# Two projections of a hybrid attention trunk: first tile and weights loaded by the phase before, waits on last stores moved, the opening's load order changed

## What is computed

```python
mod = silu(c) @ ada_w[layer] + ada_b[layer]              # six vectors of 1024, for latent and context tokens
h = rmsnorm(x, norm1_g) * (1 + scale) + shift             # the modulated input
# layer 0 (even): one input matrix, 2304 columns
qa, ka, va, qb, kb, vb = split(h @ ev_w_in)               # A: differential attention, B: windowed attention
# layer 1 (odd): one input matrix, 2336 columns
q_a, kv_a, k_r, nq, nk, nv = split(h @ od_w_in)           # C: low rank (512 + 256 + 32), D: neighbourhood
q = rmsnorm(q_a) @ wq_up ; kv = rmsnorm(kv_a) @ wkv_up    # 768 and 1024 columns
# heads are rms-normed (and turned by the rope tables), attended, projected, and followed by an MLP
```

## Time and profile before

| what | value |
|---|---|
| median of 3 runs | 3759.4 us (3757.71 to 3764.4) |
| the profiled execution, own time | 3761.42 us |
| its span in the trace | 3759.6 us |
| granted TensorE clock, mean | 0.961 |
| busy: PE, DVE, ACT, POOL | 93%, 58%, 36%, 5% |
| moved by DMA | 366.45 MB, mean 97 GB/s |

### The profile page before, as it was taken

One profiled execution on the slowest core, in us unless ns is written; L12 is line 12 of the kernel. 1 busy time (PEld: TensorE's weight loads), 2 busy tenths in 40 slices (PEclk: granted clock), 3 DMA queues, 4 the chain that ended last, 5 costly groups with the idle time before them and its releaser, 6 DMA issues. The chain is left out here.

```text
span 3759.6 us, 47907 instructions
## 1 busy us (share of the span) xinstructions
PE 3489.7 (93%) x17598; PEld 2847.5 (76%) x17598; DVE 2175.2 (58%) x3197; ACT 1339.8 (36%) x2435; POOL 185.1 (5%) x188
## 2 busy tenths in 40 slices
PE   6989898998999999999979799799899899999998
PEld 3867666886888888888858587577687678888887
DVE  5869665885755444554464355688787453333333
ACT  4533344664511111111145455566466331111111
POOL 1110300000300000000001000000000010000000
PEclk8999898998999999999989899899899999999999
DMA  6657465224322212222233444433363311111112
GB/s 222 203 201 240 120 133 135 57 75 124 90 79 58 63 57 71 69 68 58 68 101 135 167 131 123 98 73 86 65 127 76 113 51 48 47 50 50 51 50 68
DMA packets 433093, 366.45 MB, mean 97 GB/s; under 512 B 104469, under 2 KB 375077, under 8 KB 427813
## 3 DMA queue, kind: packets, MB, share of 16 engines
q1 hardware_dynamic: 432933, 364.36, 34.4%
HBM read 276.60 MB, written 87.69 MB: 97 GB/s over the span
## 5 line engine op out<-in xcount | busy, mean ns | idle before, releaser
L2470 DVE SCALAR_TENSOR_TENSOR xT<-ps,mods,xT 128x1024 f32<-128x1024 f32 x192 | 189.4, 1014 | 357.0 <-PE ps L2712 357.0
L3050 DVE TENSOR_TENSOR e_plain<-e_plain 128x1280 f32<-128x1280 f32 (+1 forms) x64 | 87.0, 1359 | 482.1 <-ACT e_plain L2899 482.1
L2712 PE MATMUL ps<-e_gh,e_w2h 128*128 128x512 f32 x1280 | 352.0, 372 | 5.9 <-DVE e_w2l L2988 3.6
L2712 PE MATMUL ps<-e_gl,e_w2h 128*128 128x512 f32 x1280 | 349.1, 370 | 0.0
L2712 PE MATMUL ps<-e_gh,e_w2l 128*128 128x512 f32 x1280 | 349.0, 370 | 0.0
L2899 ACT ACTIVATE e_plain<-ps 128x1280 f32<-128x1280 f32 (+1 forms) x64 | 72.7, 1135 | 722.9 <-PE ps L2712 718.8
L2712 PE MATMUL ps<-e_hl,e_w1h 128*128 128x512 f32 (+1 forms) x1200 | 327.2, 370 | 0.0
L2712 PE MATMUL ps<-e_hh,e_w1l 128*128 128x512 f32 (+1 forms) x1200 | 327.2, 370 | 0.0
L2712 PE MATMUL ps<-e_hh,e_w1h 128*128 128x512 f32 (+1 forms) x1200 | 327.2, 370 | 0.0
L2712 PEld LDWEIGHTS ps<-e_gh,e_w2h 128*128 128x128 f32 x1280 | 222.3, 188 | 55.2 <-DVE e_gl L3054 8.0
L2847 ACT CAST e_w2h<-e_raw 128x512 fp32r<-128x512 f32 x128 | 79.4, 620 | 495.5 <-PE ps L2712 495.5
(11 more groups left out here) (418 smaller groups left out, 7580.8 us busy)
## 6 DMA issues: line engine op xcount, KB each, us to landing
e_raw<-in_mlp_w SPq DMA_DIRECT2D x64, 512.0 KB, 4.2
e_raw<-in_mlp_w SPq DMA_DIRECT2D x128, 256.0 KB, 2.9
rstd<-in_ada_w SPq DMA_DIRECT2D x64, 384.0 KB, 3.4
e_raw<-in_w_out SPq DMA_DIRECT2D x40, 512.0 KB, 4.0
qkC<-pc_stage SPq DMA_DIRECT2D x72, 192.0 KB, 2.7
hT<-pb_hb SPq DMA_DIRECT2D x10, 1024.0 KB, 5.7
pa_hb<-hT SPq DMA_DIRECT2D x10, 1024.0 KB, 7.1
qkA<-pa_stage SPq DMA_DIRECT2D x20, 512.0 KB, 3.7
```

Of the source, the lines that this page charges most:

```text
L2470: ins = k.nc.vector.scalar_tensor_tensor(out=x, in0=ps, scalar=k.mods[:, layer, gate, bass.ds(n, 1), w], in1=x, op0=ALU.mult, op1=ALU.add)
L2712: mm = pe.matmul(k.ps[:, SB * (e % 2) + b, 0:n], w[:, e % 2, f], m[:, f, c0:c0 + n], start=(f == 0 and x == 0), stop=(f == nf - 1 and x == 2))
L3050: nc.vector.tensor_tensor(g, g, g, ALU.mult).then_inc(s.sqg, 1)
```

## The change

1. `ProjectionStart` and `LowRankStart` are new objects that hold fixed SBUF places and two semaphores (weights, tile). "pb" loads the first h tile and the first six slices of "pa"; "pd" loads the first h tile and all 16 slices of "pc"'s input matrix (3.3 MB) over the columns of its own unit 0, which its last two tiles don't use, and over its raw buffers.
2. `project` no longer waits for its stores at its end. It returns a function that does, and SP of the following block calls it just before `clear_before` ("pb" to "pa", "pa" to "ab", "pd" to "pc").
3. "pc" no longer has three raw buffers: the up matrices have places of their own. It cuts three kv slices before its first `low_rank`, and PE does `products(1)` right behind `products(0)`.
4. The opening has eight places for the eight groups of `ada_w`, so that no group waits; groups and x tiles alternate, all weight slices come behind them, and the orders of PE, ACT and DVE are written anew to follow. POOL makes the rope tables first, then the base of h tile 0, and takes half of its modulation.

```diff
+class LowRankStart:
+    def load_weights(self, sp):
+        for r in range(2):
+            for f in range(KT):
+                sp.dma_start(self.raw[r][f], self.w[r][f]).then_inc(self.weights, 16)
+    def load_tile(self, sp):
+        sp.dma_start(f32(self.hb[:, 0].rearrange("p a f q -> p (a f q)")), self.h).then_inc(self.tile, 16)
@@ opening @@
-        loads = [(0, 0, 0, None), (0, 1, 1, None), (1, 0, 2, None), (1, 1, 3, None), (2, 0, 0, 0), (2, 1, 1, 1), (3, 0, 2, "dve"), (3, 1, 0, 2)]
+        steps = [("ada", (0, 0)), ("x", 1), ("ada", (0, 1)), ("x", 2), ("x", 3), ("tables", 0), ("ada", (1, 0)), ("ada", (2, 0)), ("x", 4),
+                 ("ada", (2, 1)), ("x", 5), ("ada", (1, 1)), ("x", 6), ("ada", (3, 0)), ("x", 7), ("ada", (3, 1)), ("x", 8), ("x", 9)]
@@ opening, sync @@
-                for x in range(KT, len(slices)):
+                for x in range(len(slices)):
                     fetch_w(x)
@@ opening, tensor @@
+                ada(0, 0)
+                turn_x(1)
+                ada(0, 1)
+                turn_x(2)
+                turn_x(3)
+                ada(1, 0)
+                turn_rows(0)
+                turn_x(4)
+                ada(1, 1)
+                spread(0)
+                turn_x(5)
+                turn_x(6)
+                ada(2, 0)
+                turn_rows(1)
+                turn_x(7)
+                ada(2, 1)
+                vector_sums()
+                turn_rows(2)
+                turn_x(8)
+                turn_x(9)
+                spread(1)
                 spread(2)
@@ opening, scalar @@
+                    if x == 0:
+                        act.wait_ge(s.ada, 2)
...
-                    for f in range(KT):
+                    for f in range(KT // 2):
                         a = nc.scalar.activation(made.h[:, f], made.h[:, f], ACT.Identity, ...)
                     a.then_inc(s.fmod, 1)
                     act.wait_ge(s.fmod, 1)
+                    act.wait_ge(s.fmodp, 1)
                     nc.scalar.copy(made.hb[:, 0, 0], made.h[:]).then_inc(s.ht, 1)
...
+                for t in (5, 6, 7):
+                    take_x(t)
+                    square(t)
+                root(1)
+                square(8)
+                cut(0)
                 rows_out(2)
-                for x in range(4, RAW):
+                for x in (1, 2, 3):
                     cut(x)
                 modulate()
+                for t in (8, 9):
+                    take_x(t)
+                square(9)
+                root(2)
+                for x in (4, 5, 6, 7):
+                    cut(x)
                 take_rstd(1)
@@ opening, gpsimd @@
+                pool.wait_ge(s.base, 1)
+                pool.wait_ge(s.modd, 4)
+                pool.wait_ge(s.m0, 2)
+                for f in range(KT // 2, KT):
+                    a = nc.gpsimd.tensor_scalar(made.h[:, f], made.h[:, f], k.mods[:, 0, 1, f, 0:1], k.mods[:, 0, 0, f, 0:1], ALU.mult, ALU.add)
+                a.then_inc(s.fmodp, 1)
@@ project, sync @@
+                    if begun is None or x >= RAW:
+                        sp.dma_start(raw[:, x % RAW, 0:u.width], w_dram[...]).then_inc(wr[x % RAW], 16)
                     if x == RAW - 1:
+                        if stores_before is not None:
+                            stores_before(sp)
                         k.phases.clear_before(sp)
...
+                    if begins is not None and n == first_of[NT - 2] and not NG:
+                        sp.wait_ge(s.mm, first_of[NT - 2])
+                        sp.wait_ge(s.wlo, NW)
+                        begins.load_weights(sp)
+                    if begins is not None and n == first_of[NT - 1]:
+                        sp.wait_ge(s.mm, last_of[NT - 2] + 1)
+                        sp.wait_ge(hs[0], 16 * NT // 2)
+                        begins.load_tile(sp)
+                        if NG:
+                            sp.wait_ge(s.aacc, 2 * NG * KT)
+                            begins.load_weights(sp)
...
-                for p in range(2):
-                    sp.wait_ge(qd[p], 16 * ((len(head_jobs) + 1 - p) // 2))
-                    if value_jobs:
-                        sp.wait_ge(vd[p], 16 * ((len(value_jobs) + 1 - p) // 2))
-                    if keeps_h:
-                        sp.wait_ge(hs[p], 16 * NT // 2)
@@ project_low_rank, sync @@
-                fetch_h(0)
-                for x in range(len(slices)):
-                    fetch_w(x)
...
+                stores_before(sp)
+                for r in range(2):
+                    for f in range(RT[r]):
+                        sp.dma_start(up_raw[r][:, f], u_dram[r][f]).then_inc(wu[r], 16)
+                sp.dma_start(rope, k.ins["rope32"]).then_inc(s.ropec, 16)
+                fetch_h(1)
+                k.phases.clear_before(sp)
@@ project_low_rank, tensor @@
                 products(0)
+                products(1)
@@ project_low_rank, scalar and vector @@
-                for x in range(KT):
+                for x in range(KT + KV_EARLY):
                     cut(x)
                 low_rank(0)
```

More of the change, by code:

```diff
@@ L272, in __init__ @@
         self.rope = tile("rope", [P, 2, NT, HD])
-        last = units[-1]
-        assert prepared == len(units) - 1 and last.width == 512
-        self.spare = nc.alloc_sbuf_tensor_at(f"{name}_spare", [P, 2 * KT, n_cols], F32, offset=self.base)[:, :, last.c0:last.c0 + 512]
+        first, last = units[0], units[-1]
+        assert prepared == len(units) - 1 and first.width == last.width == 512
+        spare = nc.alloc_sbuf_tensor_at(f"{name}_spare", [P, 2 * KT, n_cols], F32, offset=self.base)
+        self.spare, self.spare_first = [spare[:, :, u.c0:u.c0 + 512] for u in (last, first)]
     def hold(self, nc, st, name):
@@ L369, in _ @@
                 sp.dma_start(brows[:], i["ada_b"].rearrange("l (k p) -> (l k) p", p=P)).then_inc(s.rows, 16)
-                for t in range(1, XB):
-                    fetch_x(t)
-                for y, (n, g, where, free) in enumerate(loads):
-                    if free == "dve":
-                        sp.wait_ge(s.aacc, 2 * GF)
-                    elif free is not None:
-                        sp.wait_ge(s.ada, free + 1)
-                    c = (n % 2) * HALF
-                    sp.dma_start(made.spare[:, GF * where:GF * where + GF], ada_w[n // 2, :, GF * g:GF * g + GF, c:c + HALF]).then_inc(aw_sem[where], 16)
-                    if y == 3:
+                for what, n in steps:
+                    if what == "x":
+                        fetch_x(n)
+                    elif what == "ada":
+                        n, g = n
+                        c = (n % 2) * HALF
+                        sp.dma_start(group(n, g), ada_w[n // 2, :, GF * g:GF * g + GF, c:c + HALF]).then_inc(aw_sem[2 * n + g], 16)
+                    else:
                         for j in hu:
@@ L523, in _ @@
                 square(0)
-                for t in range(1, XB):
+                take_x(1)
+                square(1)
+                rows_out(0)
+                for t in (2, 3):
                     take_x(t)
@@ L725, in turned_after, with landed @@
         return [n - LAG] if n - LAG in nth_head else []
+    def landed(x):
+        return wr[x % RAW], 16 * (x // RAW + (0 if begun is not None else 1))
     rest = [n for n in head_jobs if n + LAG >= N]
@@ L801, in fetch_vectors @@
                     sp.dma_start(raw[:, x % RAW], a_dram[a_group[a // KT], a % KT]).then_inc(wr[x % RAW], 16)
-                if not keeps_h:
+                if not keeps_h and begun is None:
                     fetch_h(0)
@@ L850, in products @@
                     if n == first_of[t]:
-                        if not keeps_h:
-                            pe.wait_ge(hl[t % 2], 16 * (t // 2 + 1))
+                        if begun is not None and t == 0:
+                            pe.wait_ge(begun.tile, 16)
+                        elif not keeps_h:
+                            pe.wait_ge(hl[t % 2], 16 * (t // 2 + (0 if begun is not None and t % 2 == 0 else 1)))
                         elif t >= tiles_ready:
@@ L921, in cut @@
                         x, u = nth_slice[j, f], units[j]
-                        act.wait_ge(wr[x % RAW], 16 * (x // RAW + 1))
+                        if begun is not None and x < RAW:
+                            act.wait_ge(begun.weights, 16 * RAW)
+                        else:
+                            act.wait_ge(*landed(x))
                         nc.scalar.copy(wh[:, f, u.c0:u.c0 + u.width], raw[:, x % RAW, 0:u.width]).then_inc(s.whi, 1)
@@ L1041, in vector_part @@
                     x, g, f = NW + a, a // KT, a % KT
[L1042 removed]
+                    dve.wait_ge(*landed(x))
                     if f:
@@ L1184, in project_low_rank @@
         gain = [k.rstd[:, 1152:1152 + D], sb("gain1", [P, D])[:]]
+        qh_at = next_free(nc)
+        qh = sb("qh", [P, 2, H, 2, D], F32R)
+        stage_at = next_free(nc)
+        stage = sb("stage", [D, 4, 4, P])
```

(5 more changed lines are left out.)

284 lines of the change are left out of this document (161 added, 123 removed).

## The result

The changed kernel takes 3729.7 us (median of 4 runs, 3724.2 to 3731.4) against 3759.9 for the kernel before: ratio 0.9916, 95% interval 0.9898 to 0.9933. That is faster by 30 us. It lies in the range of 3708 to 3731, but only 1.3 us under its end, and 11 of the 41 us that the terms promised are missing. The profiled execution took 3730.5 us, its span is 3728.7, so the two spans differ by 30.9. Further on one execution of one kernel, `edges_even`, is left out of its median: 3989.4 us at a mean clock of 0.825, where its others have 0.959 to 0.965.

A forecast was written before the change was run, and what follows sets the result against it. PE is busy 93% of the span, so time is won only where PE stands still or its clock is low. Terms -14 - 9 - 1 - 17 = -41 gave 3718 us, range 3708 to 3731.

The forecast's parts named there:

- The opening, -14: Opening: loads stream without group waits, so "pb" starts near 60 instead of 73.84 us, -14, bounds -9 to -17.
- PE has slack there of 2 to 3 us: Opening: PE's clock may be low after its wait for the third group, but PE has 2 to 3 us to spare.
- the start of the stream: Opening: loads run at 0.403 MB per us from near 3 us, the last x tile landing near 40.5.
- rival B: Opening: x tiles released late by waits on tile 4's transposes and squares; gain 7 instead of 14, 3725; chance 0.13.
- the case that the forecast had priced at some 2 us: Opening: POOL's four modulations could each stand behind a DVE cut, ending the opening some 2 us later.
- "pb" to "pa", -9: Edge "pb" to "pa": PE starts 7.8 us earlier, the last slice comes 8.8 earlier; -9, ends -7 and -10.
- "pa" to "ab", -1: Edge "pa" to "ab": the block starts 1.1 us earlier; -1, between 0 and -1.5.
- "pd" to "pc", -17: Edge "pd" to "pc": weights and tile loaded early, first up product 17.6 us earlier; taken as -17, bounds -12 to -20.
- Rival C: Start of "pc": its tile lands late, at 2133, so the gain is 11 instead of 17; 3724; chance 0.12.
- D: Slower: the queue serves mixed streams at about half of 403 GB/s, opening +9, in all about +5, 3764; chance 0.02.
- E: No effect: the shift is given back further on as DVE or a store paces "pa" and "pc"; 3759; chance 0.02.
- all else keeps its length: Phases behind the edges: a shift of the first tile should shift the rest, with later phases unchanged in length.

The follow-up runs named there:

- edges_even: Kernel before with only the edges "pb" to "pa" and "pa" to "ab" new, opening and edge to "pc" as before: -8.4 us by medians.
- opening_only: Kernel before with only the new opening and the moved "pb" weight issues, every edge as before: -7.0 us.
- half-width run: Changed kernel with PE's six conditioning half groups at 256 of their 512 columns: 3721.1 us (2 runs).
- late_clear: Changed kernel with the store wait and clears of "pa" moved on SP from behind its sixth weight slice to behind the twelfth: 3722.8 us.
- warm_pc: Changed kernel with POOL's wait for DVE's first low part, "pa"'s clears behind its twelfth slice, and 28 unread products at the start of "pc": 3724.8 us.
- warm_open: Changed kernel with unread products in the opening, 12 ahead of the fourth half group and 28 ahead of the second batch's spread: 3726.6 us.
- waits_moved: Changed kernel with both small edits: POOL's wait for DVE's first low part in "pb", and "pa"'s clears behind its twelfth slice: 3725.5 us.
- after_pool_waits: Changed kernel with POOL's product for tile 2 in "pb" waiting for DVE's first low part of tile 1: 3726.3 us.

## Why the prediction was right, and by how much each step was off

**The opening, -14: measured -7.0, in the profile -8.6.** ACT's queue from the row copy on was right: from `rows_out(2)` to the end of the last cut I had 16.6 us, measured 16.5 (47.92 to 64.41). The rate of a full stream was right too, 393 to 407 GB/s. The step that failed is "PE has slack there of 2 to 3 us". It had none. I had priced a half group at four records; there are eight, each 0.43 at full clock, 3.6 us. The row that showed it was in the trace of before (48 records for 24 products). PE ends its third pair at 47.9; I had ACT reach its row copy near 43.2 (41.4, a square, a cut), and the whole miss stands at that copy, 4.7 us.

Of the 4.7 us, 2.9 are the lower clock in one half group, as the run without that fall shows (44.99). The rest, 1.8 us, can't be given to the price alone: at the full clock weight slice 0 lands at 44.1, just ahead of ACT's `cut(0)`, so the transfers alone would hold the row copy until 44.7. I had x 9 land near 40.5 and slice 0 soon after, from a full rate since 3 us; with the slow windows ahead of 18 us x 9 lands at 43.4 and slice 0 at 44.1 even where nothing else is late (opening_only). So a second step was off, the start of the stream, by some 1.5 us, and it is hidden behind the first. The half-width run shows that PE was the path, and what comes next behind it.

Part of rival B came as well: in the changed kernel x 9 was released at 40.3 and landed at 44.9, because PE and so ACT's squares were late. But B had that as the cause, and here it is a consequence that held nothing: `cut(0)` started at 47.30 and did not wait for its slice. That the time is B's (3725) and not mine is no credit to either sum.

POOL's half cost 1.59 beyond ACT's, where I took 1. It is the case that the forecast had priced at some 2 us for all four modulations: the first of them stood 1.3 us behind DVE's cuts (1.76 against 0.45 us), the other three did not.

**"pb" to "pa", -9, and "pa" to "ab", -1: measured -8.0 and -1.3, together -8.4 by medians.** The part that I derived from PE's own start (-7.8) is right to 0.2. The extra from an earlier last slice did not show.

**"pd" to "pc", -17: measured -14.0, in the profile -15.2** (2164.03 to 2133.36 is 30.7, less 15.5 from ahead of "pc"). Rival C is refuted: the tile was there at 2126.8, I had said 2127. `products(0)` took 8.3 us instead of 7, at clock 0.5 until 2116.6; then from `low_rank(0)` to `turn_low(0)` it was 7.1 instead of 5.6, because the second rank's products wait 2.5 us for DVE's cuts; from the turn to the first up product 6.7, where I had 6.5. These three are 3.0 us too little for PE and DVE between the tile and the up products, against a miss of 2.4 in the whole term; the transfers were on time. Up to the last product of "pc" the profiles show some 16 us gained, the medians 14.0; where the other 2 go no run shows.

**Given back inside a phase.** I had held that all else keeps its length. "pb" took 5.4 more than in the profile of before: PE's wait ahead of the first turn is 2.4 longer (5.34 against 2.89), and the rest is the clock, which fell behind it after and not before. DVE's long low part is 2.2 us of that wait. What the order of the two costs in the median is not shown, as the experiments say. A part of the loss belongs to the opening itself: over the six kernels with the new opening, all products and no unread ones ahead of "pb", "pb" starts 9.1 us earlier on average than in the four with the old one, and its last product comes 7.3 earlier, near the 7.0 of the medians. So some 2 of the 9 us are given back in the first 31 us of "pb", by single profiles that spread over 5. The pair of operations was in the rows of before. I cited the rule for POOL's modulations and did not look for other pairs that the shift could bring together.

By the Trainium skill (SBUF — State Buffer, "Who interferes with whom") a DVE operation with two SBUF inputs and a GpSimd operation that reads SBUF shut each other out, and the order of issue decides which one waits. The traces agree with the first: 2.85 against 0.68 us for the same operation on DVE's side, 2.95 against 2.34 for the same one on GpSimd's. The second they can't show, for GpSimd's record is 40 ns ahead in both outcomes.

**How much was luck.** The direction of all four parts is right, and so are their mechanisms but for PE's slack. The number is not: the sum said 3718, "some +-7 around" it, and 3729.7 is 12 away. It lies in the range because the range was drawn to take in rivals B and C, whose reasons did not hold: a wait on x tiles, a late tile of "pc". One of its four runs (3731.35) lies outside it.

The remaining rivals: D would have shown 239 GB/s where 393 to 407 stand, E a phase that gives everything back. Neither came.

## What to carry to other kernels

Before you price a product, count records against products in its row: here plain f32 had two for one, and an engine with "slack" was the path. When a path is relieved, ask where the next one stands: here the transfers let 3.2 us of the opening go (47.92 to 44.70) and no more. Where an edit shifts a phase by microseconds, list the pairs of DVE and GpSimd operations that start together and stand ahead of PE; one semaphore wait settles their order, though here its worth in time could not be told from the spread. Parts of a change are best measured alone, since two profiles of single executions differed by up to 5 us, once 7, in stages that nobody had touched.

## What the runs showed that I had not expected

The granted clock differs between executions of the same instructions. Behind a DMA wait ahead of the same half group it stayed at 1.00 in one profile (a wait of 3.7 us) and fell to 0.5 in another (3.0 us), for 2.9 us. In the opening of three kernels (late_clear, warm_pc, warm_open) it fell between 48 and 52 us though PE had stood in no wait for the 10 us before:

```profile
48.00:50.00 2.00, 2.00 (x16) 1.99 (x16) 1.71 (x6) 1.44 (x4) 1.00 (x1) 0.73 0.44 122
```

(late_clear, columns as in rows 2.) And a stretch filled with unread products kept the clock at 1.00 in that stretch, but bought nothing in the end: -4.9 us by the end of "pa", +11.4 in "pc". The fastest medians of kernels that leave nothing out, 3722.8 to 3726.3 (late_clear, warm_pc, waits_moved, after_pool_waits), can't be told apart; all lie 3 to 7 us below the changed kernel, 2 to 6 when each is taken against the kernel before that was measured beside it, and their intervals against it overlap the changed kernel's. For none of them is a gain in time over the changed kernel shown.
